# Eight conditioning slices of the first layer, all under its query and key projections

## The chip, the cores and the metric

The kernel runs on one core of a Trainium2 chip. The metric is the device time of one execution in microseconds. TensorE (PE in the rows) multiplies matrices, VectorE (DVE), ScalarE (ACT) and GpSimd (POOL) work element by element, and SyncE (SP) issues the loads of weights.

## What is computed

A backbone of four layers over 256 context tokens and 256 latent tokens, 1024 features each. In every layer the vectors `c` and `c_ctx` give six modulation vectors each (shift, scale and gate of the mixer, and of the feed-forward part):

```python
mx = jnp.split((silu_c @ ada_w[i] + ada_b[i])[:, None, :], 6, axis=-1)
mc = jnp.split((silu_cc @ ada_w[i] + ada_b[i])[:, None, :], 6, axis=-1)
hx = modulate_norm(xs, norm_mix[i], mx[0], mx[1])
...
xs = xs + mx[2] * yx
hx = modulate_norm(xs, norm_ffn[i], mx[3], mx[4])
xs = xs + mx[5] * conv_ffn(hx, ffn_w_up[i], ffn_w_dw[i], ffn_b_dw[i], ffn_w_down[i])
```

The mixer of layer 0 is neighbourhood attention: `q, k, v = split(h @ w_qkv)`, `q` and `k` normalized per head, attention, then `@ w_o`. `ada_w` is 4 x 1024 x 6144 in float32, so one layer's product with it reads 24 MB.

## The kernel before

**Conditioning slices.** The product with `ada_w` of one layer is cut into 12 slices of 512 output columns, 2 MB of weights each. `mod_ready` counts finished slices. Shift and scale of the mixer are slices 0 to 3 and are made before everything else; 4 and 5 are the mixer's gate, 6 to 9 shift and scale of the feed-forward part, 10 and 11 its gate. A slice goes through these steps:

- SP loads four quarters of 512 KB into `ada_ring` (`load_ada`, L357). There is one ring for one slice, so the load waits on `ada_used`, that is, on the slice before.
- `ada_slice` (L568): eight matmuls on TensorE into bank 6, each pair waiting for its quarter.
- `ada_rows` (L1134): VectorE copies bank 6 to `rows`, and counts `rows_copied`.
- `ada_cols` (L576): TensorE waits for `rows_copied` and turns `rows` into columns with four small matmuls into bank 7.
- `ada_store` (L1138): VectorE waits for these, adds the bias and writes `mod`.

**The query and key projections** (L634 to L651) are 16 tiles of 128 features, in four laps (two parts, query and key, of two laps) of four tiles, m = 0 to 3. The first two tiles of the first lap are computed together (`two_tiles`, L550), and their matmuls end at the same time. A tile is 24 matmuls (8 chunks of three: high and low halves in float32r). Three engines then follow it:

- ScalarE, per tile (L937 to L941): waits for the end of tile m on TensorE (`weights_used`), squares bank m, then splits the weights of the tile three ahead into their high half (`split`, L883, which waits for the DMA), then takes the root of the head sum of tile m-1.
- VectorE, per tile (L1243 to L1247): the low half of the same weights (`split`, L1125, which waits for ScalarE's high half), and `normed` of tile m-1: a reciprocal (L1235) and a product into `QK` (L1237) that frees the bank.
- TensorE, after tile m: `head_sum` of tile m-1 (L631).
- SP: after tile m it loads the weights of the tile four ahead, 512 KB.

Every engine works its instructions in the order in which they are written. Slices 4 to 7 stand here, one to a lap: `ada_slice` behind tile 1, `ada_rows` on VectorE at m = 2, `ada_cols` behind tile 3. SP loads the next lap's slice behind the refill of tile 1's slot.

**After them** TensorE waits until slice 7 is stored (L653), since the value projection uses banks 6 and 7, and computes the values (`tokens_major`). Attention follows, then **the output projection** (L725 to L732): eight tiles in two laps, with slices 8 to 11, one to every two tiles: `ada_slice` behind the even tile, `ada_cols` behind the odd one, and on VectorE `ada_rows` ahead of the wait for the odd tile's end (L1308). Slices of later layers stand in the feed-forward parts and are not touched. GpSimd meanwhile stages the position bias of the attention (`pairs_staged`, L425): twice twelve small loads into `rel_in` and one addition over 128 x 3072 elements (L444).

Of the kernel before, what the change touches and what calls it, by code (L numbers as in the profile page):

```python
# [141 lines left out]
def build(nc, x, ada, weights, ada_in, ada_bias, gain, na_gain, rpb, na_mask, rope, decay, dist, gn_gain,  # L142
# [3 lines left out]
    with ctx:  # L146
# [201 lines left out]
        def _(sp):  # L348
# [27 lines left out]
            for layer, p in enumerate(layers):  # L376
                if layer == 0:
                    refill(p["mix"], 4, (1,), ADA_FIRST + 1)
                    refill(p["v"], 2)
                    refill(p["o"], 2, (0, 2), ADA_FIRST + 5)  # L380
                else:
                    refill(p["mix"], (p["o"] - p["mix"]) // SLOTS)
                    if layer % 3 == 1:
                        sp.wait_ge(gn_turned, RET_VC)
                    if p["ada"]:
                        load_ada(p["ada"])
                    refill(p["o"], (p["up"] - p["o"]) // SLOTS)
# [133 lines left out]
        def _(pe):  # L521
# [102 lines left out]
            def na(layer, p):  # L624
# [9 lines left out]
                for part, tok in ((0, XT if last_layer else ALL), (1, ALL)):  # L634
                    for i, first in peeled(pe, 2):
# [5 lines left out]
                        for m in range(4):  # L641
# [3 lines left out]
                            if m:  # L645
                                head_sum(m - 1, k - 1, tok)
                            if layer == 0 and m == 1:
                                ada_slice(ADA_FIRST + 2 * part, 1, i)
                            if layer == 0 and m == 3:
                                ada_cols(ADA_FIRST + 2 * part + i)  # L650
                        head_sum(3, 8 * part + 3 + 4 * i, tok)  # L651
                if layer == 0:
                    pe.wait_ge(mod_ready, 8)  # L653
                tokens_major(p["v"], 2, p["mix_tile"] + 16)
# [70 lines left out]
                for i in bodies(pe, 2):  # L725
                    for m in range(4):
                        tile(p["mix_tile"] + 24 + m + 4 * i, m, [(Step(p["o"] + m, 4, i), C)], Hhi, Hlo, tok)
                        if layer == 0:
                            if m % 2 == 0:
                                ada_slice(ADA_FIRST + 4 + m // 2, 2, i)  # L730
                            else:
                                ada_cols(ADA_FIRST + 4 + m // 2 + 2 * i)  # L732

# [386 lines left out]
        def _(dve):  # L1120
# [106 lines left out]
            def na(layer, p):  # L1227
# [4 lines left out]
                for part, tok in ((0, XT if last_layer else ALL), (1, ALL)):  # L1232
# [7 lines left out]
                    for i in bodies(dve, 2):  # L1240
                        for m in range(4):
                            k = 8 * part + m + 4 * i
                            split(Step(p["mix"] + 8 * part + m, 4, i))  # L1243
                            if layer == 0 and m == 2:
                                ada_rows(ADA_FIRST + 2 * part + i)
                            if m:
                                normed(m - 1, k - 1, tok)  # L1247
                        if layer == 0:
                            s = ADA_FIRST + 2 * part + i
                            ada_store(s, 0, s)  # L1250
                        normed(3, 8 * part + 3 + 4 * i, tok)
# [44 lines left out]
                for c in range(C):  # L1296
                    dve.wait_ge(h_hi, p["o_ready"] + c + 1)
                    v.tensor_tensor(Hlo[:, c, tok], bank[c % 4][:, tok], Hhi[:, c, tok].bitcast(F32), ALU.subtract)\
                        .then_inc(h_ready, 1)
                if layer:  # L1300
                    projected(layer, p["o"], 1, 4, tok)
                else:
                    for i in bodies(dve, 2):
                        for m in range(4):
                            st = Step(p["o"] + m, 4, i)
                            s = ADA_FIRST + 4 + m // 2 + 2 * i
                            if m % 2:
                                ada_rows(s)  # L1308
                            dve.wait_ge(weights_used, st.n + 1)
                            residual(layer, 0, bank[m], m + 4 * i, ALL)  # L1310
                            split(st)
                            if m % 2:
                                ada_store(s, 0, s)

# [318 lines left out]
```

## Time and profile before

| | us |
|---|---|
| median of 3 runs | 2870.34 |
| lowest and highest | 2869.56 and 2878.02 |
| the profiled execution | 2863.09 |
| its span, first to last instruction | 2861.3 |
| TensorE busy | 2596.9 (91%) |
| VectorE busy | 1566.0 (55%) |
| ScalarE busy | 915.0 (32%) |
| GpSimd busy | 435.5 (15%) |

Spans and starts are microseconds from the first instruction. Busy time is the time in which an engine executes. An arrow in brackets at the end of a row tells how long the engine had stood idle and whose instruction ended that. The column PEclk is the granted clock of TensorE as a share of 2.4 GHz. The query and key projections lie from 46.67 to 169 us, the values to 219, attention to 330, the output projection from 335.85 to 390.71.

### The profile page before, as it was taken

The page shows a single profiled execution, that of the slowest core. Times are in us where ns is not written, and L with a number is a line of the kernel's source. Part 1 is how long each engine was busy: PE and PEld are TensorE (multiplying, and loading weights), DVE is VectorE, ACT ScalarE, POOL GpSimd, SP SyncE. Part 2 cuts the span into 40 slices and gives each one's busy share as a digit, 9 for nine tenths or more (in the row PEclk, how much of TensorE's full clock was granted, in tenths as well). Part 3 has the DMA queues.
Part 4 walks back from the last instruction along what each step waited for, and adds up shares of the span by engine and source line. Part 5 has one row for each costly group of instructions (what it writes and reads, how often), then busy time and mean ns, then how long its engine had stood idle before and what let it go on. Part 6 is the DMA issues. An engine that isn't in the chain of part 4 may idle for free. (4 is left out here: it accounts for less than half of the span.)

```text
span 2861.3 us, 37482 instructions
## 1 busy us (share of the span) xinstructions
PE 2596.9 (91%) x12792; PEld 2054.8 (72%) x12792; DVE 1566.0 (55%) x2183; ACT 915.0 (32%) x1326; POOL 435.5 (15%) x347
## 2 busy tenths in 40 slices
PE   6999999999999989999999983528999998899999
PEld 3777777778878748777777862416777786777999
DVE  3856554443354334345444369996545434856774
ACT  2326422222232214232222234334322222335443
POOL 5000120000200010110000237753000024001000
PEclk8999999999999999999999986768999998999999
DMA  8530155544323202324554321111444434320555
GB/s 262 178 103 15 47 183 175 170 160 140 100 85 105 90 19 84 115 92 165 169 176 147 101 74 33 37 44 59 164 159 162 168 103 112 102 73 26 156 181 182
DMA packets 95007, 337.14 MB, mean 118 GB/s; under 512 B 11984, under 2 KB 13776, under 8 KB 94800
## 3 DMA queue, kind: packets, MB, share of 16 engines
q1 hardware_dynamic: 90320, 324.28, 35.0%
q0 software_dynamic: 2880, 8.92, 1.5%
q10 hardware_dynamic: 1728, 2.85, 0.3%
q8 instruction: 55, 0.90, 0.1%
q14 instruction: 24, 0.20, 0.0%
HBM read 334.95 MB, written 1.05 MB: 117 GB/s over the span
## 5 line engine op out<-in xcount | busy, mean ns | idle before, releaser
L526 PE MATMUL bank<-Hhi,Whi 128*128 128x512 f32 (+1 forms) x2240 | 857.1, 383 | 159.4 <-DVE Wlo L1125 102.7
L527 PE MATMUL bank<-Hlo,Whi 128*128 128x512 f32 (+1 forms) x2240 | 837.9, 374 | 0.0
L528 PE MATMUL bank<-Hhi,Wlo 128*128 128x512 f32 (+1 forms) x2240 | 835.7, 373 | 0.0
L1125 DVE TENSOR_TENSOR Wlo<-raw,Whi 128x1024 fp32r<-128x1024 f32 x424 | 541.8, 1279 | 409.8 <-ACT Whi L883 407.6
L883 ACT ACTIVATE Whi<-raw 128x1024 fp32r<-128x1024 f32 x424 | 448.9, 1059 | 928.3 <-DMA raw<-in_weights 927.1
L526 PEld LDWEIGHTS bank<-Hhi,Whi 128*128 128x128 f32 x2240 | 434.4, 194 | 281.8 <-DVE Wlo L1125 98.9
L528 PEld LDWEIGHTS bank<-Hhi,Wlo 128*128 128x128 f32 x2240 | 433.7, 194 | 73.2
L527 PEld LDWEIGHTS bank<-Hlo,Whi 128*128 128x128 f32 x2240 | 434.9, 194 | 71.0 <-issue 3.1
L412 POOL TENSOR_TENSOR square<-X 128x512 f32<-128x512 f32 (+1 forms) x56 | 92.1, 1644 | 1420.3 <-DVE X L1198 1420.3
L526 PE MATMUL bank<-Ghi,Whi 128*128 128x512 f32 (+1 forms) x704 | 257.5, 366 | 0.0
L528 PE MATMUL bank<-Ghi,Wlo 128*128 128x512 f32 (+1 forms) x704 | 256.2, 364 | 0.0
L527 PE MATMUL bank<-Glo,Whi 128*128 128x512 f32 (+1 forms) x704 | 254.3, 361 | 0.0
L1480 DVE TENSOR_SCALAR hb<-bank,fff 128x512 f32<-128x512 f32 (+1 forms) x88 | 65.3, 742 | 262.1 <-PE bank L528 262.1
L513 POOL TENSOR_TENSOR pooled<-pooled,prods 128x504 f32<-128x504 f32 (+5 forms) x96 | 155.7, 1622 | 79.8 <-ACT prods L1050 72.9
L1085 ACT ACTIVATE hb<-hb 128x512 f32<-128x512 f32 (+1 forms) x88 | 51.0, 580 | 322.5 <-DVE hb L1485 322.5
L528 PEld LDWEIGHTS bank<-Ghi,Wlo 128*128 128x128 f32 x704 | 132.2, 188 | 22.8
L526 PEld LDWEIGHTS bank<-Ghi,Whi 128*128 128x128 f32 x704 | 132.3, 188 | 22.4 <-DVE X L1198 2.5
L527 PEld LDWEIGHTS bank<-Glo,Whi 128*128 128x128 f32 x704 | 132.1, 188 | 22.1
L1198 DVE SCALAR_TENSOR_TENSOR X<-bank,mod,X 128x256 f32<-128x256 f32 (+1 forms) x96 | 42.7, 479 | 181.5 <-PE bank L528 181.5
L1490 DVE TENSOR_TENSOR hb<-hb,bank 128x512 f32<-128x512 f32 (+1 forms) x88 | 54.4, 619 | 114.3 <-PE bank L528 114.3
L532 PE MATMUL bank<-Whi,Hhi 128*128 128x512 f32 x256 | 100.9, 394 | 4.5 <-DVE mod L1141 4.5
L1050 ACT ACTIVATE prods<-U,cvf 128x504 f32<-128x504 f32 (+5 forms) x96 | 64.5, 702 | 119.9 <-DVEq L1398 78.2
(166 smaller groups left out, 2915.6 us busy)
## 6 DMA issues: line engine op xcount, KB each, us to landing
raw<-in_weights SPq DMA_DIRECT2D x424, 512.0 KB, 3.6
ada_ring<-in_ada SPq DMA_DIRECT2D x176, 512.0 KB, 5.9
ada_raw<-in_ada SPq DMA_DIRECT2D x16, 512.0 KB, 16.2
rel_in<-in_rpb POOLq DMA_DIRECT2D x48, 128.0 KB, 7.1
decay_t<-in_dist POOLq DMA_DIRECT2D x4, 640.0 KB, 4.3
X<-in_x ACTq DMA_DIRECT2D x1, 2048.0 KB, 9.6
out_y<-X SPq DMA_DIRECT2D x1, 1024.0 KB, 4.8
cos_sin<-in_rope ACTq DMA_DIRECT2D x1, 256.0 KB, 13.6
```

The source lines that it names most:

```text
L412: g.tensor_tensor(square[:, c_static % 2, tok], X[:, c, tok], X[:, c, tok], ALU.mult)\
L513: g.tensor_tensor(acc, acc, made, ALU.add).then_inc(tap_pooled, 1)
L526: t.matmul(dst, Whi[:, st.slot, w], hi, start=start, stop=False)
L527: t.matmul(dst, Whi[:, st.slot, w], lo, start=False, stop=False)
L528: return t.matmul(dst, Wlo[:, st.slot, w], hi, start=False, stop=stop)
L532: t.matmul(dst, hi, Whi[:, st.slot, w], start=start, stop=False)
L883: a.activation(Whi[:, st.slot, :], raw[:, st.slot, :], ACT.Copy).then_inc(hi_split, 1)
L1050: a.activation(prods[:, place, :].rearrange("p (s n) -> p s n", s=2)[:, :, lo:hi], U[:, k, :].rearrange("p (s n) -> p s n", s=2)[:, :, lo ...
L1085: a.activation(cv[:, k, tok], cv[:, k, tok], ACT.Gelu_apprx_tanh).then_inc(gelu_done, 1)
L1125: v.tensor_tensor(Wlo[:, st.slot, :], raw[:, st.slot, :], Whi[:, st.slot, :].bitcast(F32), ALU.subtract)\
L1480: v.tensor_scalar(c3, u3, f[:, 0, 1:2], f[:, 0, 3:4], ALU.mult, ALU.add).then_inc(ffn_tap, 1)
L1490: v.tensor_tensor(cv[:, k, tok], cv[:, k, tok], bank[m][:, tok], ALU.mult)\
```

## The change

All eight slices 4 to 11 now stand in the query and key projections, two to a lap. `ada_slice` stands behind tiles 0 and 2, `ada_cols` behind tiles 1 and 3. VectorE copies the rows at m = 1 and m = 3, behind the split of that same m, and stores the columns behind `normed` of tile m-1. SP loads a slice behind the refill of tile 1's slot and another behind that of tile 3's. The output projection holds no slice, and uses the function that the other layers use. TensorE waits for all 12 slices ahead of the value projection.

```diff
--- before.py
+++ after.py
@@ -375,9 +375,9 @@
             load_ada(ADA_FIRST)
             for layer, p in enumerate(layers):
                 if layer == 0:
-                    refill(p["mix"], 4, (1,), ADA_FIRST + 1)
+                    refill(p["mix"], 4, (1, 3), ADA_FIRST + 1)
                     refill(p["v"], 2)
-                    refill(p["o"], 2, (0, 2), ADA_FIRST + 5)
+                    refill(p["o"], 2)
                 else:
                     refill(p["mix"], (p["o"] - p["mix"]) // SLOTS)
                     if layer % 3 == 1:
@@ -644,13 +644,13 @@
                                 tile(p["mix_tile"] + k, m, [(steps[m], C)], Hhi, Hlo, tok)
                             if m:
                                 head_sum(m - 1, k - 1, tok)
-                            if layer == 0 and m == 1:
-                                ada_slice(ADA_FIRST + 2 * part, 1, i)
-                            if layer == 0 and m == 3:
-                                ada_cols(ADA_FIRST + 2 * part + i)
+                            if layer == 0 and m % 2 == 0:
+                                ada_slice(ADA_FIRST + 4 * part + m // 2, 2, i)
+                            if layer == 0 and m % 2:
+                                ada_cols(ADA_FIRST + 4 * part + m // 2 + 2 * i)
                         head_sum(3, 8 * part + 3 + 4 * i, tok)
                 if layer == 0:
-                    pe.wait_ge(mod_ready, 8)
+                    pe.wait_ge(mod_ready, ADA_SLICES)
                 tokens_major(p["v"], 2, p["mix_tile"] + 16)
 
 
@@ -725,11 +725,6 @@
                 for i in bodies(pe, 2):
                     for m in range(4):
                         tile(p["mix_tile"] + 24 + m + 4 * i, m, [(Step(p["o"] + m, 4, i), C)], Hhi, Hlo, tok)
-                        if layer == 0:
-                            if m % 2 == 0:
-                                ada_slice(ADA_FIRST + 4 + m // 2, 2, i)
-                            else:
-                                ada_cols(ADA_FIRST + 4 + m // 2 + 2 * i)
 
             def retention(p):
                 for i, first in peeled(pe, 4):
@@ -1241,13 +1236,13 @@
                         for m in range(4):
                             k = 8 * part + m + 4 * i
                             split(Step(p["mix"] + 8 * part + m, 4, i))
-                            if layer == 0 and m == 2:
-                                ada_rows(ADA_FIRST + 2 * part + i)
+                            s = ADA_FIRST + 4 * part + m // 2 + 2 * i
+                            if layer == 0 and m % 2:
+                                ada_rows(s)
                             if m:
                                 normed(m - 1, k - 1, tok)
-                        if layer == 0:
-                            s = ADA_FIRST + 2 * part + i
-                            ada_store(s, 0, s)
+                            if layer == 0 and m % 2:
+                                ada_store(s, 0, s)
                         normed(3, 8 * part + 3 + 4 * i, tok)
                 dve.wait_ge(rel_ready, 2 * j + 2)
                 tokens_major(p["v"], 2, V)
@@ -1297,20 +1292,7 @@
                     dve.wait_ge(h_hi, p["o_ready"] + c + 1)
                     v.tensor_tensor(Hlo[:, c, tok], bank[c % 4][:, tok], Hhi[:, c, tok].bitcast(F32), ALU.subtract)\
                         .then_inc(h_ready, 1)
-                if layer:
-                    projected(layer, p["o"], 1, 4, tok)
-                else:
-                    for i in bodies(dve, 2):
-                        for m in range(4):
-                            st = Step(p["o"] + m, 4, i)
-                            s = ADA_FIRST + 4 + m // 2 + 2 * i
-                            if m % 2:
-                                ada_rows(s)
-                            dve.wait_ge(weights_used, st.n + 1)
-                            residual(layer, 0, bank[m], m + 4 * i, ALL)
-                            split(st)
-                            if m % 2:
-                                ada_store(s, 0, s)
+                projected(layer, p["o"], 1, 4, tok)
 
             def retention(p):
                 cos, sin = cos_sin[:, 0, :], cos_sin[:, 1, :]
```

On TensorE, at the start of the query projection, behind the two tiles computed together. `ada_ring` holds the slice's weights, `na_sq` the squared tile, `rows` the copied rows; the matmul of L631 waits for `qk_squared`, those of L566 for `ada_loaded`, the first of L580 for `rows_copied`. Before:

```order
L527 MATMUL bank<-Hlo,Whi 128x512
L528 MATMUL bank<-Hhi,Wlo 128x512
L631 MATMUL bank<-na_sq,one_head 128x512
L566 MATMUL bank<-ada_ring,csilu 32x512 x8
L526 MATMUL bank<-Hhi,Whi 128x512
L527 MATMUL bank<-Hlo,Whi 128x512
```

And now:

```order
L527 MATMUL bank<-Hlo,Whi 128x512
L528 MATMUL bank<-Hhi,Wlo 128x512
L566 MATMUL bank<-ada_ring,csilu 32x512 x8
L631 MATMUL bank<-na_sq,one_head 128x512
L580 MATMUL bank<-picker,rows 128x2 x4
L526 MATMUL bank<-Hhi,Whi 128x512
```

The slice has moved ahead of the head sum, and the small matmuls of `ada_cols`, which wait for `rows_copied`, have come in between the head sum and tile 2; before, they came behind tile 3.

On VectorE, in the loop over the laps of the query projection, from m = 1 on (`Wlo` is the low half of weights, `na_root` the reciprocal, `QK` the normalized tile). Before:

```order
L1125 TENSOR_TENSOR Wlo<-raw,Whi 128x1024 [waits hi_split]
L1234 REGISTER_ALU
L1235 RECIPROCAL na_root<-na_root 128x512 [waits qk_root]
L1237 ISA [waits qk_rstd]
L1237 SCALAR_TENSOR_TENSOR QK<-bank,qk_gain,na_root 128x512
L1124 REGISTER_ALU
L1125 TENSOR_TENSOR Wlo<-raw,Whi 128x1024 [waits hi_split]
L1135 REGISTER_ALU
L1136 COPY rows<-bank 128x512 [waits ada_used]
```

And now (the function of L1125 has become L1120, and so on):

```order
L1120 TENSOR_TENSOR Wlo<-raw,Whi 128x1024 [waits hi_split]
L1130 ISA
L1131 COPY rows<-bank 128x512 [waits ada_used]
L1229 REGISTER_ALU
L1230 RECIPROCAL na_root<-na_root 128x512 [waits qk_root]
L1232 ISA [waits qk_rstd]
L1232 SCALAR_TENSOR_TENSOR QK<-bank,qk_gain,na_root 128x512
L1135 REGISTER_ALU
L1136 ISA [waits cols_made]
L1136 REGISTER_ALU
L1136 TENSOR_TENSOR mod<-bank,bias_ada 128x8
```

The copy of the rows has moved from behind the split of m = 2 to behind the split of m = 1, ahead of the reciprocal; the store follows in the same iteration. The same again at m = 3:

```order
L1125 TENSOR_TENSOR Wlo<-raw,Whi 128x1024 [waits hi_split]
L1234 REGISTER_ALU
L1235 RECIPROCAL na_root<-na_root 128x512 [waits qk_root]
L1237 ISA [waits qk_rstd]
L1237 SCALAR_TENSOR_TENSOR QK<-bank,qk_gain,na_root 128x512
L1140 REGISTER_ALU
L1141 ISA [waits cols_made]
L1141 REGISTER_ALU
L1141 TENSOR_TENSOR mod<-bank,bias_ada 128x8
L1235 RECIPROCAL na_root<-na_root 128x512 [waits qk_root]
L1237 ISA [waits qk_rstd]
L1237 SCALAR_TENSOR_TENSOR QK<-bank,qk_gain,na_root 128x512
```

```order
L1120 TENSOR_TENSOR Wlo<-raw,Whi 128x1024 [waits hi_split]
L1130 REGISTER_ALU
L1131 COPY rows<-bank 128x512 [waits ada_used]
L1229 REGISTER_ALU
L1230 RECIPROCAL na_root<-na_root 128x512 [waits qk_root]
L1232 ISA [waits qk_rstd]
L1232 SCALAR_TENSOR_TENSOR QK<-bank,qk_gain,na_root 128x512
L1135 REGISTER_ALU
L1136 ISA [waits cols_made]
L1136 TENSOR_TENSOR mod<-bank,bias_ada 128x8
```

At m = 3 the rows were not copied before; now they are, behind that tile's split.

## Rows read from the trace of the kernel before

**Rows 1.** Busy time, clock and DMA of five stretches (columns in the first line)

```profile
core 0: us, PE busy (x) PEld busy (x) DVE busy (x) ACT busy (x) POOL busy (x), PEclk, DMA share, GB/s
65.99:83.83 17.84, 17.84 (x81) 11.71 (x80) 12.20 (x8) 5.44 (x8) 6.16 (x9) 0.95 1.02 236
83.83:112.12 28.29, 28.29 (x130) 20.77 (x129) 22.68 (x15) 10.02 (x14) 5.54 (x1) 1.00 0.53 180
140.41:166.49 26.08, 26.08 (x119) 19.28 (x118) 19.83 (x13) 6.59 (x10) 0.00 (x0) 1.00 0.46 154
166.49:173.77 7.28, 2.77 (x14) 1.46 (x12) 6.63 (x7) 3.87 (x5) 0.00 (x0) 1.00 0.25 72
335.85:390.71 54.86, 54.86 (x281) 40.18 (x282) 16.68 (x28) 7.42 (x7) 22.73 (x14) 1.00 0.60 204
```

**Rows 2.** Timeline (start, us), TensorE, the later half of the second lap

```profile
96.12 1.92 PE L566 MATMUL bank<-ada_ring,csilu 128*32 128x512 f32 x16
...
97.97 0.50 PE L526 MATMUL bank<-Hhi,Whi 128*128 128x512 f32 x1
...
109.91 1.02 PE L631 MATMUL bank<-na_sq,one_head 128*128 128x512 f32 x2
...
110.77 0.95 PE L580 MATMUL bank<-picker,rows 128*128 128x2 f32 x8
...
111.58 1.10 PE L631 MATMUL bank<-na_sq,one_head 128*128 128x512 f32 x2
```

**Rows 3.** Timeline, behind the end of one query tile, three engines

```profile
103.57 1.02 PE L631 MATMUL bank<-na_sq,one_head 128*128 128x512 f32 x2
...
104.26 1.05 ACT L883 ACTIVATE Whi<-raw 128x1024 fp32r<-128x1024 f32 x1
...
106.49 0.68 DVE L1136 COPY rows<-bank 128x512 f32<-128x512 f32 x1
```

**Rows 4.** Timeline, the first lap, five engines

```profile
67.83 1.93 PE L566 MATMUL bank<-ada_ring,csilu 128*32 128x512 f32 x16
...
69.69 0.50 PE L526 MATMUL bank<-Hhi,Whi 128*128 128x512 f32 x1
...
71.41 1.06 ACT L883 ACTIVATE Whi<-raw 128x1024 fp32r<-128x1024 f32 x1 [4.43 <-DMA raw<-in_weights]
...
72.51 1.23 DVE L1125 TENSOR_TENSOR Wlo<-raw,Whi 128x1024 fp32r<-128x1024 f32 x1 [4.75 <-ACT Whi L883]
...
82.62 6.75 POOL L444 TENSOR_TENSOR rel<-rel_in,mask 128x3072 f32<-128x3072 f32 x1 [11.68 <-DMA rel_in<-in_rpb]
...
88.41 2.04 DVE L1125 TENSOR_TENSOR Wlo<-raw,Whi 128x1024 fp32r<-128x1024 f32 x1 [4.63 <-ACT Whi L883]
```

**Rows 5.** DMA issues from 64 to 84 us: count, KB each, median us to landing

```profile
ada_ring<-in_ada SPq DMA_DIRECT2D x4, 512.0 KB, 13.3
```

**Rows 6.** Timeline, SP's queue: the issue of one slice's four loads

```profile
98.25 1.91 SPq L362 DMA_DIRECT2D ada_ring<-in_ada  x4
```

**Rows 7.** Windows of 1 us at the end of that load

```profile
107.00:108.00 1.00, 1.00 (x6) 0.84 (x5) 1.00 (x2) 0.00 (x0) 0.00 (x0) 1.00 0.11 45
```

**Rows 8.** Timeline, TensorE's wait ahead of the value projection

```profile
173.77 0.80 PE L532 MATMUL bank<-Whi,Hhi 128*128 128x512 f32 x1 [4.51 <-DVE mod L1141]
```

**Rows 9.** Windows (columns as in rows 1) behind waits of TensorE

```profile
395.00:396.00 1.00, 0.89 (x2) 0.30 (x2) 0.05 (x1) 0.00 (x0) 0.00 (x0) 0.79 0.04 16
174.00:177.00 3.00, 3.00 (x8) 2.33 (x9) 2.97 (x1) 0.00 (x0) 0.00 (x0) 0.50 0.00 0
988.00:992.00 4.00, 4.00 (x12) 2.01 (x12) 0.00 (x0) 0.00 (x0) 3.70 (x6) 1.00 0.00 0
1168.00:1172.00 4.00, 3.95 (x9) 3.15 (x10) 1.23 (x1) 1.04 (x1) 0.00 (x0) 0.50 0.99 389
```

**Rows 10.** TensorE's waits over the span: us in total, times, longest us

```profile
PE bank L526 <- DVE Ylo L1380: 3.9, 1, 3.9
PE bank L750 <- DVE Vr L1224: 3.1, 1, 3.1
```

## What the change was predicted to do

> **What bounds the kernel now.** I read four views. First, windows over the stages that the diff touches [rows 1]: in a lap of the query and key projections TensorE is busy for 28.29 of 28.29 us, in the output projection for 54.86 of 54.86, at full clock in both. VectorE comes next in a lap with 22.68 us, ScalarE has 10.02, the loads a share of 0.53. So TensorE is the bound in both stages; whatever it executes more or waits for there is added to the time, and whatever is taken from it is gained. It stands idle only at the border to the value projection: 4.51 us, ended by VectorE's store of slice 7 [rows 8].
>
> Second, TensorE's own timeline gives the prices of a slice [rows 2]. From the start of `ada_slice` to the next tile it is 97.97 - 96.12 = 1.85 us, from the start of `ada_cols` to the next head sum 111.58 - 110.77 = 0.81, from the end of a tile through its head sum to what follows 110.77 - 109.91 = 0.86.
>
> Third, what the other engines do behind the end of a tile [rows 3]. Here lies the point of the change. The tile m = 2 ends at 103.57; ScalarE squares it and starts on the weights of three tiles ahead at 104.26; VectorE's low half of these follows, and then the copy of the slice's rows, from 106.49 to 107.17. **The copy is done 3.6 us behind the end of the tile of its own iteration**, although the slice itself was ready long before. In the kernel before nobody minds: the copy stands at m = 2, and `ada_cols` comes behind tile 3, more than 3 us later.
>
> **What moves onto the path.** Now the copy stands at m = 1 and m = 3, behind the split, which waits for ScalarE, which waits for the end of that same tile. And TensorE has `ada_cols` right behind that same tile and its head sum. TensorE gets there 0.86 us behind the tile's end, the copy is done at 3.6, with about 0.06 for the signal: **a wait of 2.8 us, twice in every lap**. Behind the waiting matmul the next tile is queued, so all of it is time. Nothing is gained in return, since the slice's matmuls take the same 1.85 us wherever they stand.
>
> The sum, relative to the profiled execution:
>
> - *Second and third lap.* One more slice, 1.85; one more set of columns, 0.81; two waits of 2.8. That is 8.3 each, 16.5 together. VectorE has one more copy and store, under 0.9 us on 22.7, so it doesn't become late.
> - *First lap.* Two tiles end together at about 66, and ScalarE's second split waits for a weight load until 71.41, as the small loads of the position bias go on beside it [rows 4]. VectorE's low half starts at 72.51, the copy about 1.15 later, and is done at 74.3; with the columns tile 2 starts at 75.2 where it was 69.69: 5.5. TensorE is then idle for some 5.6 us, and its clock falls. What that costs: behind the wait of 3.9 us [rows 10] and behind the one of 4.51 it runs at 0.50, that is 1.2 GHz, for 4 and for 3 us at least [rows 9], and half of such a stretch is lost, 1.5 to 2.7; I take 2.2, as the wait is longer than these. The slice behind tile 2 adds 1.85. Its load: beside the bias loads four quarters took 13.3 us to land [rows 5]; issued at about 68 it is there between 81 and 86, and wanted at 84: 0 to 2, I take 0.5. The wait at m = 3, 2.8. Last, GpSimd's long addition runs from 82.6 to 89.4, where VectorE will want to make the low half; the one made beside it took 2.04 us where 1.23 is usual [rows 4]: 0 to 0.9, I take 0.5. Sum 13.3.
> - *Fourth lap.* As the second without the wait at m = 3: there TensorE has to wait for the store of the last slice in any case, and this comes one copy later, 0.6. So 8.3 - 2.8 + 0.6 = 6.1.
> - *Output projection.* It loses four slices and three sets of columns that stood between tiles: -(4 x 1.85 + 3 x 0.81) = -9.8. The fourth set stood behind the last tile, beside the wait for the norm, and brings nothing.
> - *The clock at the steady waits.* A wait of 3.1 us [rows 10] left it at 1.00 [rows 9], one of 3.9 did not. The new waits are 2.8, but the columns behind them are matmuls of two columns, and behind the norm's small matmuls and short gaps the clock fell too, by 395 [rows 9]. Six waits (one in the first lap, four, one) with 0 to 2.2 each: 0 to 13. The wait of 3.1 is the nearest row in length, so most shouldn't fall; I take 4.
> - *The clock at the values.* Before, the values start at 0.50. Now the idle time ahead of them is cut into 2.8 and 2.6 by the columns. 0 to -1.7; I take 0.
>
> Together 13.3 + 16.5 + 6.1 - 9.8 + 4 = 30. Against its own time that is 2863.1 + 30 = 2893; the median of the runs shown is 2870.3, 7 us above the profiled execution, so the forecast for the median is **2900 us**.
>
> **A page on that addition.** Behind the row of 2.04 us: the Trainium skill, "SBUF — State Buffer", section "SBUF: two separate sides", says that VectorE and GpSimd share one pair of ports, which an instruction of GpSimd holds to its end against a VectorE instruction with two SBUF inputs. The row agrees as far as it goes: it ends 1.1 us behind the addition. By the rule the low half of the first lap, wanted at about 85, would stand until 89.4, and the copy behind tile 3 would come some 0.9 later than 2.8 says; by the usual duration it would come no later. The sum would be 30.5 by the rule and 29.6 by the usual duration.
>
> **Rivals.**
>
> - *The clock falls at every new wait.* For it: 2.8 us of idleness and 0.8 of tiny matmuls lie side by side, as long as the stretch ahead of 395. Against it: the wait of 3.1 left it alone. Price 13 instead of 4: 2909.
> - *The slice's load is late.* There is one ring, so a load can only follow the slice before, and now there is one in every two tiles. The load shown was issued at 98.25 and the DMA was done shortly after 107 [rows 6, 7], 9.2 us, with another weight load in between. It is now issued 0.4 behind an odd tile's end and wanted 0.86 + 2.8 + 0.81 + 5.5 + 0.86 = 10.8 behind it. So it is hidden with a microsecond to spare, and only because of the wait at the columns; without this it would be wanted at 8.0. Should it land 1.5 us later seven times: 2911.
> - *The copy comes in time, and the change breaks even.* If TensorE found the rows copied when it gets to the columns, only work would be moved: 4 x 2.66 - 9.8, about +1. It decides at 0.86 us behind the tile's end. Against it: the chain of rows 3, three instructions of 1.05, 1.23 and 0.68 us one behind the other, none of which can start ahead of the tile's end except the last, and this one is written behind the others. About 2871.
> - *VectorE is the bound, and the output projection's gain stays whole.* If a lap was as long as VectorE's work, TensorE's waits in it would cost nothing and the kernel would be faster by 9.8: 2861. It decides where VectorE's 22.7 plus 0.9 reach 28.3; it is 4.7 short.
>
> That the change doesn't do what it says is excluded by the order of instructions: the copy is behind the split and the columns are behind the odd tile.
>
> **How the numbers follow.** Forecast 0.65; clock 0.14; loads 0.10; break-even 0.08; VectorE 0.03. The range reaches from the forecast with every open term at its low end (no clock loss at the steady waits or in the first lap, a faster start of the values: about 22 on the median, or somewhat less on a lower run like the profiled one) to the second and third case with some of both: 2884 to 2914. A measurement of this kernel can tell about 0.3% from no change, 8.6 us. Slower by more: 0.89. Within it: 0.08. Faster: 0.03.
>
> **What would show it.** In the profile after: waits of TensorE ended by VectorE's copy of the rows, about 7 of them, six of 2.8 us and the first over 5; laps of 36.6 us instead of 28.3; the output projection at 45 us; `ada_slice` without a wait for DMA but in the first lap; PEclk at 1.00 in most of the second to fourth lap. I would be wrong if there are no such waits, if `ada_slice` waits for its quarters in each lap, or if laps are over 39 us, where the clock would be the cause.

## The result and the profile after

| | before | changed |
|---|---|---|
| median of four runs | 2870.57 us | 2906.95 us |
| least to most | 2869.56 to 2878.02 | 2898.72 to 2911.24 |
| profiled execution, its own time | 2863.09 | 2909.15 |
| its span | 2861.3 | 2907.3 |
| granted clock over the span | 0.950 | 0.943 |

The ratio is 1.0118, with an interval of 1.0089 to 1.0147: slower by 1.2%, 36 us on the medians. The forecast was 2900, between 2884 and 2914.

TensorE's waits over the whole span of the changed kernel (us in total, times, longest us) have a line that the kernel before did not have, the first one here. It is the wait that the prediction was about, and the second line is what is left of the wait of [rows 8]:

```profile
PE bank L580 <- DVE rows L1131: 31.0, 8, 12.6
...
PE bank L532 <- DVE mod L1136: 1.6, 1, 1.6
```

The same stretches as in [rows 1], from the start of one lap's first tile to the next's, now of the changed kernel (the first begins with the end of the two tiles, the fourth ends with the first matmul of the values, the fifth is the output projection):

```profile
core 0: us, PE busy (x) PEld busy (x) DVE busy (x) ACT busy (x) POOL busy (x), PEclk, DMA share, GB/s
69.49:108.76 39.27, 24.02 (x105) 15.75 (x105) 22.21 (x12) 7.33 (x11) 7.10 (x2) 0.78 0.45 137
108.76:147.42 38.66, 33.40 (x154) 22.98 (x153) 22.29 (x17) 8.59 (x12) 0.00 (x0) 0.96 0.45 162
147.42:187.69 40.27, 35.01 (x155) 24.01 (x153) 22.29 (x17) 8.59 (x12) 0.00 (x0) 0.92 0.46 158
187.69:229.14 41.45, 34.63 (x155) 22.96 (x153) 24.92 (x20) 10.10 (x14) 0.00 (x0) 0.92 0.50 178
391.38:434.99 43.61, 43.61 (x193) 36.12 (x193) 14.05 (x21) 7.43 (x7) 22.68 (x14) 1.00 0.28 85
```

Read the second row against 83.83 to 112.12 of [rows 1]. TensorE was busy for all of a lap of 28.29 us; it is now idle for 38.66 - 33.40 = 5.26, two waits of 2.63, and what it is busy with has grown by 5.1. Of that some 3 are the second slice. The rest is the clock: 0.96 where it was 1.00. The changes of the laps are 21.4 (39.27 against 17.84), 10.4, 12.0 and 8.1 (41.45 against 26.08 + 7.28), together 51.9. The output projection gives back 54.86 - 43.61 = 11.25, of which 0.6 are lost again directly behind it: from its start to the first matmul of the feed-forward part it is 53.24 us where it was 63.90. The stage ahead of all this begins 3.05 later and takes 0.45 more, ahead of anything that was changed. The sum is 44.2 of the 46.0 by which the spans differ; the values, with 0.16, and all that comes behind the output projection, with 1.7 (the 0.6 among them), are the rest.

A steady wait, second half of the first lap. This is the timeline of the changed kernel (start, us, engine, line, operation, tiles; in brackets the idle time before and what ended it), to be held against [rows 3]:

```profile
103.66 1.02 PE L631 MATMUL bank<-na_sq,one_head 128*128 128x512 f32 x2
...
104.35 1.05 ACT L878 ACTIVATE Whi<-raw 128x1024 fp32r<-128x1024 f32 x1
...
105.43 1.22 DVE L1120 TENSOR_TENSOR Wlo<-raw,Whi 128x1024 fp32r<-128x1024 f32 x1 [3.01 <-ACT Whi L878]
106.57 0.68 DVE L1131 COPY rows<-bank 128x512 f32<-128x512 f32 x1
...
107.31 1.05 PE L580 MATMUL bank<-picker,rows 128*128 128x2 f32 x8 [2.63 <-DVE rows L1131]
```

The chain is that of [rows 3], link by link: head sum, high half, low half, copy, and the copy ends 107.25 - 103.66 = 3.59 behind the tile. Only now TensorE stands at its end.

The first lap went worse than forecast. Its first wait, in the same kernel's timeline:

```profile
75.61 1.06 ACT L878 ACTIVATE Whi<-raw 128x1024 fp32r<-128x1024 f32 x1 [4.67 <-DMA raw<-in_weights]
...
76.66 6.69 POOL L444 TENSOR_TENSOR rel<-rel_in,mask 128x3072 f32<-128x3072 f32 x1 [6.76 <-DMA rel_in<-in_rpb]
76.70 7.73 DVE L1120 TENSOR_TENSOR Wlo<-raw,Whi 128x1024 fp32r<-128x1024 f32 x1 [4.98 <-ACT Whi L878]
84.35 0.68 DVE L1131 COPY rows<-bank 128x512 f32<-128x512 f32 x1
...
85.09 1.86 PE L580 MATMUL bank<-picker,rows 128*128 128x2 f32 x8 [12.62 <-DVE rows L1131]
```

GpSimd's addition began 0.04 us ahead of VectorE's low half, and the low half took 7.73 us instead of 1.22. It ended 1.08 behind the addition's end (76.66 + 6.69 = 83.35, against 84.43), which is about its own usual length, so it seems to have got nothing done while the addition ran. Its input was there, since ScalarE's high half ended at 76.67; a late load of the weights is not what held it. In the kernel before the addition came at 82.62 and fell on a low half for which nobody waited [rows 4].

Last the clock, in windows of the changed kernel (columns as above), behind the first wait and behind two of the steady ones:

```profile
85.00:93.00 8.00, 7.91 (x23) 6.56 (x24) 4.11 (x4) 0.00 (x0) 0.00 (x0) 0.50 0.01 2
...
148.00:151.00 3.00, 3.00 (x8) 2.32 (x7) 2.86 (x4) 0.69 (x1) 0.00 (x0) 0.50 0.97 395
...
206.50:209.50 3.00, 3.00 (x18) 2.62 (x19) 3.00 (x1) 0.00 (x0) 0.00 (x0) 1.00 0.91 347
```

Behind four of the six steady waits that have a tile behind them TensorE ran at 0.50, that is 1.2 GHz, for 3.2 to 3.4 us; behind the waits that ended at 107.31 and 206.39 it ran at 1.00. A fall costs half of such a stretch, 1.6 us. Behind the first wait the low clock lasted until about 93.

### The profile page after: what moved, and what is told of

The parts are those of the page before. It is cut to its first block and busy times, and to the rows that moved or that the text cites. A ratio compares the mean times of both kernels' runs of the same rounds, so it can differ in the third digit from the quotient of the medians.

```text
span 2907.3 us, 37472 instructions
## 1 busy us (share of the span) xinstructions
PE 2614.2 (90%) x12792; PEld 2064.3 (71%) x12792; DVE 1572.1 (54%) x2183; ACT 914.6 (31%) x1326; POOL 434.5 (15%) x347
## 5 line engine op out<-in xcount | busy, mean ns | idle before, releaser
L1120 DVE TENSOR_TENSOR Wlo<-raw,Whi 128x1024 fp32r<-128x1024 f32 x424 | 547.7, 1292 | 454.9 <-ACT Whi L878 452.6
```

What stands on the lines that cost most here:

```text
L1120: v.tensor_tensor(Wlo[:, st.slot, :], raw[:, st.slot, :], Whi[:, st.slot, :].bitcast(F32), ALU.subtract)\
```

## Experiments

All ratios are to the kernel before, run on the same chip in the same session, with the 95% interval. Where a diff starts from the changed kernel, its ratio is to be held against that kernel's 1.0118.

### The changed kernel again

> The changed kernel as it is, to stand beside the others on this chip. Theory (TensorE waits for the copy of the rows eight times, 31 us in all, of which 12.6 in the first lap, and its clock falls behind some of the waits): again 1.012 of the kernel before, 2905 us, seven waits of 2.6 us and one of 5 to 13, by whether GpSimd's long addition starts ahead of VectorE's low half or behind it. Rival (a difference of the start of the program): the waits would be there but the time would scatter as much as the whole difference.

No edit. Measured 1.0113 (1.0092 to 1.0134), median 2900.99. The first figure therefore stands, and this profile shows how the first lap varies. Timeline of this run, first lap:

```profile
56.24 6.73 POOL L444 TENSOR_TENSOR rel<-rel_in,mask 128x3072 f32<-128x3072 f32 x1 [13.11 <-DMA rel_in<-in_rpb]
...
60.20 4.99 DVE L1120 TENSOR_TENSOR Wlo<-raw,Whi 128x1024 fp32r<-128x1024 f32 x2 [3.81 <-ACT Whi L878]
...
65.85 1.87 PE L580 MATMUL bank<-picker,rows 128*128 128x2 f32 x8 [3.67 <-DVE rows L1131]
```

Here the bias loads landed at other moments, so the two additions met other low halves: they made waits of 3.67 and 6.12 in place of 12.62 and 2.63. The other six waits are 2.63 again. The clock was at 0.50 behind all five of these that have a tile behind them; one window:

```profile
153.00:156.00 3.00, 3.00 (x8) 2.32 (x7) 2.33 (x3) 0.00 (x0) 0.00 (x0) 0.50 0.99 374
```

### The copy ahead of the split

```diff
-                            split(Step(p["mix"] + 8 * part + m, 4, i))
                             s = ADA_FIRST + 4 * part + m // 2 + 2 * i
...
                                 ada_rows(s)
+                            split(Step(p["mix"] + 8 * part + m, 4, i))
```

> Only VectorE's copy of the slice's rows is moved, from behind the split of m = 1 and m = 3 to ahead of it. Theory (the wait at the columns comes from the copy's place behind the split): the waits of TensorE for the rows go from 31 us to under 1, laps come down from 39-40 us to about 31, no clock loss in them, and the time comes back to that of the kernel before within 0.3% (2871, ratio 1.000). Rival (the slice's load is late once the wait is gone, since it is wanted 8.0 us behind its issue): TensorE waits for ada_ring 1 to 2 us seven times instead, laps of 33 us, ratio 1.003 to 1.005. Rival (VectorE's load as such is the cause): the waits stay, ratio 1.012.

Measured 1.0031 (1.0017 to 1.0044). No wait for the rows is left, and with them went about three quarters of the loss. That is the theory's wait, taken away by the order of two steps of VectorE's program, with the same work on every engine. But 1.000 was not reached. The timeline of the first lap and a window over the third show what took the place:

```profile
80.48 4.87 PE L566 MATMUL bank<-ada_ring,csilu 128*32 128x512 f32 x16 [3.26 <-DMA ada_ring<-in_ada]
```

```profile
125.28:158.54 33.26, 33.26 (x155) 22.23 (x153) 22.21 (x17) 8.59 (x13) 0.00 (x0) 1.00 0.53 189
```

The slice waits for its load in the first lap, and a slice's matmuls take 2.2 to 3.1 us from there on where they took 1.92. I read that as quarters that land one after the other under them, and the next run, in which only the loads are issued earlier, bears it out. This is the second rival, the late load, and it comes true only now. The prediction had said so: with the wait the slice is wanted 10.8 behind the tile's end, without it at 8.0, and the load takes 9.2. The clock stayed at 1.00, in a lap that is again all busy.

### The copy ahead of the split, and the load one tile earlier

```diff
-                    refill(p["mix"], 4, (1, 3), ADA_FIRST + 1)
+                    refill(p["mix"], 4, (0, 2), ADA_FIRST + 1)
```

This comes on top of the edit before; SP issues a slice's loads one tile earlier.

> The kernel with the rows copied ahead of the split, with SP's loads of a slice moved from behind the refills of slots 1 and 3 to behind those of slots 0 and 2, so that a load is issued as soon as the slice before is used. Theory (the 0.3% that stay with the rows first are late loads: 3.3 us and more in the first lap and 0.2 to 1.3 us in a slice of the others): ada_slice takes 1.9 us everywhere but in the first lap, laps come from 32.2 to 33.3 down to 31.0, the time 4 to 7 us below that kernel, ratio about 1.001. Rival (the rest is the clock in the first laps, or VectorE, which is busy most of the lap): the same time as that kernel, ratio 1.003.

Measured 1.0021 (1.0007 to 1.0034). All slices but the first lap's take 1.92 us again. Windows over the second and third lap and the output projection:

```profile
92.56:123.84 31.28, 31.28 (x154) 22.00 (x153) 21.16 (x16) 8.47 (x12) 0.00 (x0) 1.00 0.55 191
123.84:155.12 31.28, 31.28 (x154) 22.00 (x153) 22.21 (x17) 8.59 (x13) 0.00 (x0) 1.00 0.56 204
356.60:401.81 45.21, 45.21 (x193) 37.27 (x194) 14.05 (x21) 7.43 (x7) 22.68 (x14) 0.96 0.27 82
```

The first two rows give the work of a lap without any wait: it grows by 31.28 - 28.29 = 3.0, not 2.66. The output projection shrinks by 9.65 here, but its clock is at 0.96, with some 3 us at 0.50 at its start; at full clock, in the changed kernel, it shrank by 11.25. In this profile the first lap takes 5.2 more than before, the other three 3.0 each, and 14.2 - 9.65 is a loss of 4.5 us, or 0.16%. Work alone is 4 x 3.0 - 11.25 = 0.75 of that. Another 2.2 lie in the first lap, 1.5 of them in waits (0.76 for quarters of a load, 0.78 for the rows), and 1.6 are the clock of the output projection. The medians are 6.0 us apart.

### The store ahead of the normalization too

```diff
-                            if m:
-                                normed(m - 1, k - 1, tok)
                             if layer == 0 and m % 2:
                                 ada_store(s, 0, s)
+                            if m:
+                                normed(m - 1, k - 1, tok)
```

On top of the two edits before. The values wait for the last slice's store, and now it does not stand behind a reciprocal.

> As the one before, and VectorE also stores a slice ahead of normed of tile m-1 instead of behind it. The last store ends TensorE's wait of 4.5 us ahead of the value projection. Theory (that wait is the reciprocal and the product that stand ahead of the store, 4.15 us): the values start 3.2 us behind the last tile's end instead of 7.3, the clock stays at 1.00 there, 5 to 6 us less, ratio 0.999. Rival (the wait is then for a bank or for the rows of weights): it gets only 1 to 2 us shorter, ratio 1.001.

Measured 0.9995 (0.9984 to 1.0006). TensorE's last wait ahead of the values, 4.51 us in [rows 8], is gone, and the values begin at full speed, a matmul of 0.50 us where one of 0.80 stood:

```profile
185.96 0.50 PE L532 MATMUL bank<-Whi,Hhi 128*128 128x512 f32 x1 [0.36 <-DVE mod L1136]
```

### The store ahead of the normalization in the kernel before

```diff
+                            if layer == 0 and m == 3:
+                                s = ADA_FIRST + 2 * part + i
+                                ada_store(s, 0, s)
                             if m:
                                 normed(m - 1, k - 1, tok)
-                        if layer == 0:
-                            s = ADA_FIRST + 2 * part + i
-                            ada_store(s, 0, s)
```

> The kernel before, with only the store of slices 4 to 7 moved ahead of normed of tile 2. Theory (as above): the wait of 4.5 us ahead of the values goes to about 0.5, the clock stays up, 4 to 6 us faster than the kernel before, ratio 0.998. Rival (the store now waits for the columns and holds up VectorE): laps get longer by 0.5 us or more and the ratio is 1.000.

Measured 0.9953 (0.9935 to 0.9971). A gain from the same edit without the changed placement: so what the last kernel won is not due to the slices. The wait fell from 4.51 to 0.36, and the values take 42.99 at clock 1.00 where they took 44.53:

```profile
170.53:213.52 42.99, 42.99 (x189) 35.58 (x190) 18.85 (x15) 8.78 (x9) 2.22 (x4) 1.00 0.27 87
```

That is 4.2 + 1.5 = 5.7 us, 0.2%; the ratio says 0.47%. What the other part is I did not find out: this profiled execution, with a span of 2861.8, is no shorter than that of the kernel before, while the median is 2857.49. The same edit gained 6.5 us on the medians of the changed placement (2875.55 to 2869.01) and 4.0 on top of the pieces below (2849.49 to 2845.51), so the 5.7 of the rows is nearer to its worth than the ratio here.

This kernel and that of the experiment before it differ in the placement, and in the two edits that keep the copy and the loads of the latter in time. Their medians are 11.5 us apart, 2869.01 with the slices moved and 2857.49 without.

### Something for TensorE to do in the wait

```diff
                             if layer == 0 and m % 2:
+                                pe.wait_ge(tile_free, p["mix_tile"] + k + 2)
+                                for _ in range(3):
+                                    t.matmul(bank[(m + 1) % 4][:, tok], one_head[:, :], na_sq[:, (m - 1) % 2, tok],
+                                             start=True, stop=True)
                                 ada_cols(ADA_FIRST + 4 * part + m // 2 + 2 * i)
```

Three matmuls more stand ahead of each `ada_cols` in the changed kernel; the next tile overwrites what they leave in the bank, and the added `wait_ge` makes sure that the bank is free. The wait stays as long as it is, only it is filled, so that the price of the clock comes out alone.

> The changed kernel with three more matmuls (0.86 us each, 2.6 in all) ahead of each set of columns. They write the next tile's bank, which that tile overwrites, so they fill the 2.63 us in which TensorE waits for the rows and change no result. Theory (what stands in the trace as slow tiles behind the waits is the clock at 1.2 GHz, about 1.6 us for each of four or five waits): PEclk is 1.00 in laps 2 to 4, these are 36.5 to 37 us instead of 38.7 to 40.3, the time is 6 to 9 us below the changed kernel, ratio about 1.009. Rival (tiles are slow there because of the loads that run beside them): slow tiles and laps stay, ratio 1.011 or more.

Measured 1.0085 (1.0065 to 1.0106), 0.3% under the changed kernel; the intervals overlap, so the ratio alone is not enough. The trace is plain. The added matmuls, and the window over the second lap:

```profile
111.23 2.74 PE L652 MATMUL bank<-na_sq,one_head 128*128 128x512 f32 x6
```

```profile
96.92:134.04 37.12, 37.00 (x167) 24.11 (x165) 22.30 (x17) 8.60 (x12) 0.00 (x0) 1.00 0.47 167
```

With something running in the wait, the clock stays at 1.00 and a lap takes 37.1 in place of 38.7 and 40.3, one fall and two falls of 1.6 each. That is 5.8 above the 31.28 of a lap without waits: 5.26 for the two waits, 0.2 for the fillers, which take 2.74 where the wait is 2.63, and 0.4 for which I have no row. So the idle wait does cost the clock, and the larger part of the loss is the wait itself.

### GpSimd's addition in pieces, changed kernel

```diff
-                    g.tensor_tensor(rel[:, some * half:some * (half + 1), :, :].rearrange("p h a k -> p (h a) k"),
-                                    rel_in[:, :, ::-1],
-                                    mask[:, None, :].to_broadcast([P, some * 6, GRID_W]), ALU.add)\
-                        .then_inc(rel_ready, 1)
+                    for piece in range(8):
+                        h = some * half + piece
+                        last = g.tensor_tensor(rel[:, h, :, :], rel_in[:, 6 * piece:6 * piece + 6, ::-1],
+                                               mask[:, None, :].to_broadcast([P, 6, GRID_W]), ALU.add)
+                    last.then_inc(rel_ready, 1)
```

One addition of 6.7 us becomes eight of about 1.

> The changed kernel with GpSimd's two additions of 6.7 us over 128 x 3072 elements cut into eight each, of 384 elements. Theory (the long addition holds VectorE's low half in the first lap, 7.7 us instead of 1.2): that low half takes under 2.5 us, the first wait for the rows is about 6 us instead of 12.6, the clock recovers earlier, the time is 7 to 10 us below the changed kernel, ratio about 1.009. Rival (the low half is late because of its weights' load): the first wait stays near 12 us, ratio 1.012.

Measured 1.0051 (1.0032 to 1.0070). In the first lap of the profiled execution the low half takes 1.22 and TensorE's wait is 3.26 in place of 12.62:

```profile
67.70 1.22 DVE L1121 TENSOR_TENSOR Wlo<-raw,Whi 128x1024 fp32r<-128x1024 f32 x1 [2.14 <-ACT Whi L879]
68.85 0.68 DVE L1132 COPY rows<-bank 128x512 f32<-128x512 f32 x1
...
69.59 1.05 PE L581 MATMUL bank<-picker,rows 128*128 128x2 f32 x8 [3.26 <-DVE rows L1132]
```

These rows alone do not show that the pieces did it. The pieces of the first addition had ended at 63.54, and those of the second began at 86.02, so none ran beside this low half. A low half beside pieces stands in the last kernel below: 1.93 us from 60.72, among pieces that ran from 55.38 to 64.47. With the long wait gone the load of the first lap's second slice is late here too, by two waits of 2.40 and 2.67.

The kernel gained 0.6%, some 17 us, which is more than the first lap had to give. This profile can't show where: its execution took 2902.74, the longest of the seven, and their median is 2886.34. The next run shows a part of it.

### GpSimd's addition in pieces, kernel before

The same edit of the kernel before.

> The kernel before with GpSimd's two long additions cut into eight each. Theory (a long addition holds VectorE's instruction with two inputs in SBUF to its end, also where the last chunks of the normed input are made, ahead of the first two tiles): TensorE's wait of 4.9 us at 63 goes under 1.5, the clock stays up behind it, 5 to 8 us faster than the kernel before, ratio 0.998. Rival (the pieces gain only in the changed kernel, where VectorE's copy is on the path): ratio 1.000.

Measured 0.9928 (0.9912 to 0.9944), far above the 0.2% expected. The same function runs in a later layer, and there the addition stood on the path. First the kernel before, its timeline there:

```profile
2416.17 7.14 POOL L444 TENSOR_TENSOR rel<-rel_in,mask 128x3072 f32<-128x3072 f32 x1 [4.09 <-DMA rel_in<-in_rpb]
...
2417.46 7.33 DVE L1178 SCALAR_TENSOR_TENSOR Hlo<-square,mod,Hhi 128x256 fp32r<-128x256 f32 x4
...
2424.05 0.58 PE L526 MATMUL bank<-Hhi,Whi 128*128 128x256 f32 x1 [6.26 <-DVE Hlo L1178]
```

And the kernel with pieces:

```profile
2419.62 9.76 POOL L446 TENSOR_TENSOR rel<-rel_in,mask 128x384 f32<-128x384 f32 x8 [4.24 <-DMA rel_in<-in_rpb]
...
2422.42 0.38 PE L527 MATMUL bank<-Hhi,Whi 128*128 128x256 f32 x1 [1.34 <-DVE Hlo L1179]
```

The pieces take longer together, 9.76 against 7.14, and let VectorE in between. One more wait for `Hlo`, of 1.08, follows. A second wait of this kind there, 7.00 us and ended by VectorE's `QK`, stood behind a low half of 6.34 beside the layer's second addition; it is 0.24 now. That one says little for the pieces: they began only at 2447.42, when the place was past, where the whole addition had begun at 2440.53. In the first layer the one ahead of the first tiles fell from 4.86 to 1.3. Over the whole span the waits for `Hlo` and `QK` fell by 13 us, from 39.0 and 7.0 to 31.6 and 1.5. The median fell by 21, but this profiled execution is only 6.5 shorter than that of the kernel before; for the rest I have no row. I had looked for the addition's effect in the first layer only.

### Both edits in the kernel before, and both in the kernel with the slices moved

The first is the kernel before with the store ahead of the normalization and the additions in pieces, the second the changed kernel with the copy and the store first, the loads early and the additions in pieces.

> Both edits on the kernel before: the store of slices 4 to 7 ahead of normed, and the additions in pieces. Theory (they lie at two places, 100 us apart, and add up): ratio 0.995 times that of the pieces alone, about 0.993. Rival (the first lap ends at the slowest of several things, the weights' load next): no better than the store alone, 0.995.

> The changed placement, all eight slices in the query and key projections, with everything found: rows copied and columns stored early, loads issued early, additions in pieces. Theory (the placement itself costs a little: 3.0 us a lap and 2 to 5 us in the first lap against 9.7 to 11 us in the output projection): 3 to 6 us slower than the kernel before with the same two edits, ratio about 0.996. Rival (with all waits gone the placement is worth something, since the output projection runs without interruption): equal to or below it, 0.993 or less.

Measured 0.9919 (0.9906 to 0.9932), median 2845.51, for the first, and 0.9954 (0.9939 to 0.9968), median 2856.19, for the second. The product of the two single ratios would be 0.988, but that counts the 0.9953 in full, of which the rows had explained less than half; on top of the pieces the store is worth 4.0 us. The first is the fastest kernel of this study, 25 us under the kernel before, without any of the changed placement.

The pair answers the question of the change with nearly every wait taken out of it. Windows over the query and key projections and over the output projection, first the kernel without the change:

```profile
45.94:162.80 116.86, 116.49 (x513) 84.95 (x513) 90.18 (x79) 40.86 (x61) 26.68 (x28) 0.97 0.60 170
323.34:379.04 55.70, 55.70 (x288) 40.98 (x289) 17.05 (x29) 7.42 (x7) 22.70 (x14) 1.00 0.60 210
```

And the kernel with it:

```profile
46.22:181.62 135.40, 131.46 (x608) 91.74 (x608) 93.59 (x87) 40.98 (x61) 24.91 (x28) 0.96 0.68 207
343.71:388.96 45.25, 45.24 (x192) 37.27 (x193) 14.05 (x21) 7.43 (x7) 22.69 (x14) 0.96 0.27 81
```

The window of the output projection without the change ends 0.8 later than the other windows of that stage, behind the last set of columns; up to the last tile's end, at 378.23, it is 54.89. So it is plus 18.5 and minus 9.6: 8.9 us in the profiles, 10.7 on the medians. Of the 18.5, 15.0 are busy time and 3.6 idle time, two waits for the rows in the first lap, 0.61 and 2.98. The longer one stands behind a low half for whose weights VectorE had waited 6.38 us. Of the busy time 12.0 are the work of four laps; most of the other 3.0 is the clock, which is at 0.50 behind that wait until 88.9. The output projection now runs at 0.96: at its start the clock is at 0.50 for about 3 us behind a wait of 2.02 for VectorE's `Hlo`, so 1.6 of its gain were lost here. This fall comes and goes with the slices in either place. Of the profiled executions it is in six of the eight with the slices moved, but not in that of the changed kernel itself, and in two of the four with the slices where they were.

## Why the prediction was right

The time, the sign and the mechanism came as forecast: waits for the copy's rows, one long and the others alike (seven, where six were forecast: the last one too, ahead of the values, is seen as a wait for the copy), laps with 5.3 us of idle time each, the output projection shorter by four slices. One sign that had been named for being wrong did show: the third lap took 40.27 us, over the 39 that were the mark for the clock as a cause, and the clock was a cause, though a smaller one than the waits. That the forecast of +30 lies so near to the +36 of the medians is in part luck, since the profiled pair differs by 46. Moving the copy ahead of the split (1.0118 to 1.0031) shows that this order of VectorE's program, and nothing in the slices' own work, made most of the loss.

- **The steady wait.** 2.8 forecast, 2.63 measured, seven times. The chain was right: the copy is done 3.59 behind the tile, and TensorE starts to wait 1.02 behind it (107.31 - 2.63 - 103.66) where the forecast had 0.86.
- **The work.** 2.66 per slice forecast. Without waits a lap grew by 3.0, and the output projection lost 9.65 to 11.25, with 9.8 forecast. Part of the 0.33 lies at the seam to a head sum, which the prediction did not price: in the kernel before, a tile follows 0.46 behind the start of the head sum (75.28 to 75.74), and a slice only 0.95 behind it (95.17 to 96.12).
- **The first lap.** 13.3 forecast, 21.4 in this execution. The step that was mis-sized is the addition's: it was given 0.5 at m = 3, since the row of 2.04 [rows 4] was taken for what one usually loses beside it. Its true price depends on the moment. When the addition starts just ahead of a low half, the low half stands for the whole addition, which is 6.5 us, and it was the first low half that was hit, since the bias load landed at 76.7 and not at 82.6. The wait of 5.6 became 12.6, and the low clock behind it lasted until 93. In the second profiled run the two waits were 3.67 and 6.12, which is the forecast's 5.6 and 2.8 with 1.4 more. The behaviour is one that the page named in the prediction describes: the Trainium skill, "SBUF — State Buffer", section "SBUF: two separate sides". It says that an instruction of GpSimd keeps the ports which it shares with VectorE until it ends. By the prediction that rule was worth 0.4 us; the rows of 7.73 and of 4.99 (two low halves, of which the first ended 1.1 behind the addition) agree with it, and the mistake was to apply it only at the one place where the timeline of before had shown the meeting.
- **The fourth lap.** 6.1 forecast, 8.1 measured. Idle time is 2.3 more than before (two waits of 2.63 and one of 1.55 in place of 4.51), where 3.4 was forecast; busy time is 5.8 more, where 2.7 was forecast: the slice, a fall of the clock at the lap's start, and the low clock behind the last wait.
- **The clock.** 4 us forecast. Four falls of 1.6 in this execution, five in the second: 6.4 and 8.0. The step "most shouldn't fall", by the wait of 3.1 [rows 10] that left the clock alone, was wrong: most did. Of the first rival half came true, since a fall costs 1.6 and not 2.2. The filled wait confirms it: 37.1 against 38.7 and 40.3.
- **The clock at the values.** Taken at 0, measured 0: they start at 0.50 as before, as their first matmul takes 0.80 in both. With the whole wait gone it is 1.5.
- **The late load.** Hidden in the changed kernel, as forecast, and late as soon as the waits were gone, or only the long one in the first lap.
- **Break-even.** It was priced at +1 if only work moves, and for work alone that is right: 4 x 3.0 - 11.25 = 0.75, or 1.3 with what is lost directly behind the output projection. But in no version tried was work alone what moved. With the copy and the loads in time the change still costs 6.0, 11.5 and 10.7 us on the medians of the three pairs (early loads against the kernel before; store first; everything), of which the profiles show only the waits of the first lap and falls of the clock. What the rest is stays open.

The sum of the profiled pair: 31.0 of new waits, less 3.0 at the values; 12.0 of work; some 6.4 of clock at the steady waits and some 4 behind the first one; -11.25; 3.5 ahead of the changed place; 1.9 behind it. This is 44.6 of 46.0. The forecast of 30 was short by the first lap's 8.1 above all, by the clock at the steady waits, and by scatter outside the changed stages.

## What to carry to other kernels

A result that one engine copies for another should be copied when it is ready, ahead of work in that engine's order that waits for something later: here the order of two lines was worth 0.9%. When a wait goes, price what it hid (here a load with 1 us to spare), and look at every place at which a long instruction can meet another, not at the one where it was seen, since a DMA decides when it starts. Compare windows that end at the same instruction: one that holds a set of columns more than its partner shifts the balance by 0.8 us. A saving of waits is there to be had first: the two edits to the order and the length of instructions gained 0.8% without moving any work.

## What the runs showed of the hardware

- **One GpSimd addition can hold VectorE for its whole length.** The low half (two inputs in SBUF) took 7.73 us beside an addition of 6.69, 4.71 beside one that had 3.6 left, and 1.22 alone; each time it ended 1.08 behind the addition. In the later layer four `Hlo` instructions, two of which take 0.87 elsewhere, took 7.33 beside one. Cut in eight, the addition takes 2.6 us longer, low halves beside the pieces took 1.4 to 1.9, and the kernel is 0.7% faster.
- **The clock fell behind waits of 2.63 us with matmuls of two columns behind them** in nine of eleven cases in two runs, although it did not behind one of 3.1 in a stretch of wide matmuls [rows 9 and 10]. In the run with the addition in pieces it was at 0.50 behind five of six such waits. With wide matmuls put into the wait it stayed up in all of the three laps, and so it did with no wait there and the matmuls of two columns alone. Why it did not fall at 107.31 and 206.39 is open.
- **A load that is slightly late shows first as a longer group of matmuls.** With the copy first, the slices' groups grew from 1.92 to as much as 3.1 us in the second to fourth lap, where the list of waits has a single wait for this load, of 0.16, and a lap of 33.26 us counts as busy throughout.
